# Rank products directly behind the mask's wait, three units' column sums behind the ranks, in a routed two-layer block kernel

## The reference, cut to what matters

```python
def hierarchical_moe(hin, w_group, b_group, w_router, b_router, w_gate, w_up, w_down):
    ...
    g_w, g_idx = lax.top_k(g_prob, 1)
    ...
    e_val, e_idx = lax.top_k(e_logits, EXPERT_TOP_K)
    e_w = jax.nn.softmax(e_val, -1)
    flat_idx = g_idx * EXPERTS_PER_GROUP + e_idx
    ...
    for e in range(N_EXPERTS):
        hid = jax.nn.silu(xt @ w_gate[e]) * (xt @ w_up[e])
        y = y + gates[:, e:e + 1] * (hid @ w_down[e]).astype(jnp.float32)
```

## Time and profile before

| | us |
|---|---|
| median of three timed runs | 1268.32 |
| lowest and highest of them | 1265.24, 1273.74 |
| the profiled execution | 1266.25 |
| its span | 1264.5 |
| mean granted clock of PE in it | 0.979 |

### The profile page before, as it was taken

One profiled execution on the slowest core, in us unless ns is written; L12 is line 12 of the kernel. 1 busy time (PEld: TensorE's weight loads), 2 busy tenths in 40 slices (PEclk: granted clock), 3 DMA queues, 4 the chain that ended last, 5 costly groups with the idle time before them and its releaser, 6 DMA issues.

```text
span 1264.5 us, 17438 instructions
## 1 busy us (share of the span) xinstructions
PE 1198.5 (95%) x7154; PEld 702.5 (56%) x7155; DVE 361.2 (29%) x1017; ACT 295.0 (23%) x626; POOL 83.8 (7%) x141
## 2 busy tenths in 40 slices
PE   4799999999999999999889999999999999999997
PEld 1566644544444448764433444445878778767773
DVE  0202414322212123952521121114211344342212
ACT  2112433111000021063400000103002545542101
POOL 2000011000000001500000000000000313200000
PEclk8799999899999999999989999999999999999999
DMA  9997999999999999831889999999834433424000
GB/s 336 313 387 243 308 280 385 382 425 428 430 429 428 429 397 208 247 133 67 360 355 404 404 422 429 427 429 388 204 133 146 152 97 130 150 80 145 17 1 33
DMA packets 90371, 352.77 MB, mean 279 GB/s; under 512 B 5284, under 2 KB 7500, under 8 KB 78028
## 3 DMA queue, kind: packets, MB, share of 16 engines
q1 hardware_dynamic: 83160, 340.68, 71.6%
q0 software_dynamic: 5488, 8.12, 3.1%
q10 hardware_dynamic: 1668, 3.21, 0.7%
HBM read 350.84 MB, written 1.15 MB: 278 GB/s over the span
## 4 chain that ended last, share of the span: by engine, by line
PE 80%; DMA 13%; DVE 2%; ACT 2%; issue 2%; SPq 1%; ACTq 0%; DVEq 0%
PE bank L456 28%; PE bank L751 20%; PE bank L469 12%; DMA ring<-in_moe_w_up 10%; PE bank L723 3%; PE bank L492 3%; PE bank L772 3%; DMA ring<-in_ev_w_in 2%; PE bank L505 2%; PE bank L1016 1%; SPq L368 1%; PE bank L603 1%; PE bank L640 1%; PE bank L643 1%; PE bank L629 1%
## 5 line engine op out<-in xcount | busy, mean ns | idle before, releaser
L456 PE MATMUL bank<-arena,ring 128*128 128x256 f32 x1600 | 356.0, 384 | 6.1 <-DVE arena L1539 2.8
L751 PE MATMUL bank<-ring,arena 128*32 128x512 f32 x3072 | 339.5, 600 | 12.1 <-issue 7.1
L456 PEld LDWEIGHTS bank<-arena,ring 128*128 128x128 f32 x1600 | 305.7, 192 | 54.6 <-issue 7.1
L751 PEld LDWEIGHTS bank<-ring,arena 128*32 128x32 f32 x3072 | 102.0, 111 | 237.0 <-issue 234.3
L469 PE MATMUL bank<-ring,arena 128*128 128x512 f32 x352 | 153.7, 594 | 2.3 <-DVE arena L2378 1.5
L469 PEld LDWEIGHTS bank<-ring,arena 128*128 128x128 f32 x352 | 66.2, 190 | 83.0 <-issue 79.6
L492 PE MATMUL bank<-ring,c_rep 128*32 128x512 f32 x480 | 64.3, 667 | 11.8 <-DMA ring<-in_w_ada 10.1
L2003 DVE TENSOR_TENSOR arena<-arena,bank 128x512 f32<-128x512 f32 x16 | 11.0, 688 | 203.8 <-PE bank L751 203.8
L723 PEld LDWEIGHTS bank<-arena 128*128 128x128 f32 x512 | 60.3, 197 | 13.6 <-issue 13.3
L723 PE MATMUL bank<-arena 128*128 128x128 f32 x512 | 63.4, 284 | 1.6 <-DVE arena L1971 1.5
L1283 ACT ACTIVATE arena<-bank 128x512 f32<-128x512 f32 x16 | 9.6, 597 | 216.8 <-PE bank L751 216.8
(11 more groups left out here) (300 smaller groups left out, 926.5 us busy)
## 6 DMA issues: line engine op xcount, KB each, us to landing
ring<-in_moe_w_gate SPq DMA_DIRECT2D x32, 2048.0 KB, 14.0
ring<-in_moe_w_up SPq DMA_DIRECT2D x32, 2048.0 KB, 16.7
ring<-in_moe_w_down SPq DMA_DIRECT2D x32, 2048.0 KB, 13.8
ring<-in_w_ada SPq DMA_DIRECT2D x24, 2048.0 KB, 14.1
ring<-in_w_in SPq DMA_DIRECT2D x16, 2048.0 KB, 8.9
ring<-in_w_c SPq DMA_DIRECT2D x6, 2048.0 KB, 9.2
ring<-in_ev_w_in SPq DMA_DIRECT2D x5, 2048.0 KB, 20.2
ring<-in_od_w_in SPq DMA_DIRECT2D x5, 2048.0 KB, 19.6
```

What stands on the lines that cost most here:

```text
L456: mm = pe.matmul(ps[k0][:, t * S:(t + 1) * S], w[:, k, c:c + P], rhs[:, k, :], start=(k == 0), stop=(k == KT - 1))
L751: mm = pe.matmul(bank[col:col + CHUNK, :], lhs[:, k, col:col + CHUNK], ring[:, s0 + e, cut], start=start, stop=stop, tile_position=(0, col))
```

## The change

In `experts` of the PE program the wait for `ada_part_taken` and the three `ada_columns` move from ahead of the wait for `mask_ready` to behind the five rank products, ahead of the last `ada_main`. No instruction is added or taken away, and no other engine's program changes. It takes effect twice, once in each layer.

```diff
                 for n in range(units - 3):
                     ada_main()
-                pe.wait_ge(sem("ada_part_taken"), units_before + 4)
-                for n in range(ROUTE_SOON):
-                    ada_columns()
-
                 pe.wait_ge(sem("mask_ready"), layer + 1)
                 mask = rt[:, 512:512 + 32].rearrange("p (t e) -> p t e", e=EXPERTS)
                 pe.matmul(ps[4][:, 384:400], lt, mask[:, 0, :], start=True, stop=True)
...
                 pe.matmul(ps[4][:, 416:432], ones, mask[:, 0, :], start=True, stop=False)
                 pe.matmul(ps[4][:, 416:432], ones, mask[:, 1, :], start=False, stop=True)\
                   .then_inc(sem("rank_full"), 1)
+                pe.wait_ge(sem("ada_part_taken"), units_before + 4)
+                for n in range(ROUTE_SOON):
+                    ada_columns()
                 ada_main()
```

## The result

The changed kernel takes 1272.01 us (median of 20 executions, 1266.21 to 1275.46) against 1268.41 for the kernel before (20 executions, 1264.84 to 1273.74). The ratio is 1.0025, 95% interval 1.0014 to 1.0037: by this ratio 3.2 us slower, between 1.8 and 4.7 (the two medians themselves lie 3.6 apart). The forecast was 1.5 us slower, the rival in which the clock falls in layer 1 as well 3.2 to 5.2 (1271.5 to 1273.5).

The account below looks back on a forecast made before the run. PE was taken to hold 80% of the span and arriving weights 13%. Layer 1's +0.1 and layer 0's +1.4 gave +1.5 us, 1267.75 for the profiled execution and 1269.8 as median (chance 0.36); range 1264.0 to 1276.0.

Parts of the forecast that it names:

- the rival in which the clock falls in layer 1 as well: Layer 1's last modulation product, perhaps its gather too, runs at half clock: 1271.5 to 1273.5, written 1272.5; chance 0.24.
- The wait for the mask: PE ahead of the ranks, both layers: without the columns' cover it idles 1.24 us, bounds 1.1 and 1.5.
- DVE: In layer 1 ranks start 1.43 us earlier and so do the picks; DVE's wait shrinks from 2.82 to about 1.4.
- The copy takes the place of the picks: Ahead of the gather, ACT's copy of the last part, 1.24 us later in layer 1, becomes the last wait.
- the rival that said they would: Early ranks get through to the gather: layer 1 gains 1.43 us, layer 0 0.3; 1266.6, chance 0.09.
- Layer 1's +0.1, at full clock: Layer 1's gather, with no clock fall, starts at 626.23 instead of 626.12: net +0.1 us.
- The cases without any fall: Clock falls in neither layer: +0.1 in layer 1 and -0.3 in layer 0, 1268.1; chance 0.18.
- without any effect: Layer 1's stall ends at a fixed time and layer 0's queue has more reserve: 1268.3; chance 0.10.
- The stall of 4.08 us: PE's wait ahead of layer 1's first pair, no releaser shown; taken to move with PE, so the 0.1 stays.
- Layer 0's +1.4: Clock falls and returns as before; gather ends at 237.73 instead of 236.35, +1.4 us; bounds -0.3 and +1.4.
- the queue passes the lateness on in full: Weight stream sets each layer's end: a later first pair delays it fully; an earlier one gains about 0.3 us in layer 0.
- Theory A: From the experiments: the time is PE at half clock, as idleness, ranks and columns side by side bring more or earlier falls.

Follow-up runs that it names:

- four filled ones: Changed kernel with one 512-column product (ratios 0.9990, 0.9989) or five one-column products (1.0075, 1.0077) ahead of the mask's wait, results unused; each run twice.
- layer 1 alone: New order in layer 1 only, layer 0 as in the kernel before: 1270.04 us, ratio 1.0015 to the kernel before.
- changed, again: The changed kernel, unaltered, run a second time: 1271.59 us against 1266.88 for the kernel before, ratio 1.0026.
- layer 0 alone: New order in layer 0 only, layer 1 as in the kernel before: 1269.19 us against 1266.96, ratio 1.0015.
- four products first: Changed kernel with the last modulation product moved ahead of the mask's wait, behind its three sisters: 1266.28 us against 1268.39 for the kernel before, ratio 0.9983.
- the same, again: Last modulation product moved ahead of the mask's wait in the changed kernel, second run: 1266.27 us against 1266.88 for the kernel before, ratio 0.9986.
- and one dense product: Four products first, plus one unused 512-column product behind the first unit's columns: 1265.01 us against 1266.88 for the kernel before, ratio 0.9989.
- before, with dense product: Kernel before with one unused 512-column product between columns and ranks: 1268.41 us against 1268.39, ratio 0.9999.
- dense product in the wait: Changed kernel with one unused 512-column product ahead of the mask's wait: 1264.81 us against 1266.96 for the kernel before, ratio 0.9990.
- one unit ahead: Changed kernel with one of the three units' columns kept ahead of the mask's wait: 1267.11 us against 1268.39 for the kernel before, ratio 0.9985.
- dense in the wait, again: Changed kernel with one unused 512-column product ahead of the mask's wait, second run: 1267.22 us against 1268.39 for the kernel before, ratio 0.9989.

## Why the prediction was right or wrong

The range held, the direction was right, and the size was short: 1.5 us forecast, 3.2 measured, with 1.5 just below the interval of 1.8 to 4.7. The steps in their order:

*The wait for the mask.* Forecast 1.24 us of idleness; 1.17 in both layers. Right.

*DVE.* The ranks were to come 1.43 us earlier; they came 1.46 earlier (12.28 to 10.82), and DVE's wait shrank to 1.38, as forecast. Right.

*The copy takes the place of the picks.* Right in both layers: the picks were done 5.5 us ahead of the gather in layer 1 and 4.2 in layer 0 (228.53 to 232.73), and ACT's L1172 released it. This is why nothing of the early ranks got through, and the rival that said they would is refuted. The sum of +0.1 at full clock was never seen, since no stage of the new order ran without a fall.

*Layer 1's +0.1, at full clock.* This is the step that failed. It supposed that layer 1 would keep the full clock it had in the one profile before. All 14 profiled stages with the whole change, the wait filled or not, had a fall in them (two in each of the two profiles of the changed kernel and of the four filled ones, one in each single-layer run), and so had all ten stages of the orders tried besides; only the old order had stages without one, two of four. The gather came 3.95 us later, where the prediction allowed 0.3, and the first pair 6.35. That profile is the worst of its kind. In layer 1, against 17.24, 26.00 and 271.62 us from the logits before:

| profile | clock in the stage | gather late by | first pair late by | experts over late by |
|---|---|---|---|---|
| changed | fall | 3.95 | 6.35 | 4.83 |
| changed, again | fall | 3.37 | 3.84 | 1.39 |
| layer 1 alone | fall | 3.37 | 3.78 | 1.31 |
| layer 0 alone (layer 1 in the old order) | fall | 1.62 | 3.81 | 1.69 |

So the old order with a fall ended its layer 1 as late as the new order did in two of its three profiles. The one profile before, on which the forecast was built, had no fall in this place, and the forecast also left out the fall under the first pair, of which the 0.91 from 640 to 645 was a sign. The rival with this mechanism, 1271.5 to 1273.5, holds the measured 1272.01. The cases without any fall (1268.1) and without any effect (1268.3) lie below the interval.

*The stall of 4.08 us* ahead of layer 1's first pair moves with PE, as taken: 4.20 after, and 4.47 with layer 1 alone; over all profiles it is 3.7 to 4.6. In the kernel before a transfer of instructions lies within it, between 631 and 632 us; its cause was not tried.

*Layer 0's +1.4.* The first pair was 1.22 us later, near the forecast, but not by the recorded steps. They let the clock fall at the old time, under the columns, which would take 4.84 us, and start the gather 21.24 us from the logits. The fall came 1.22 us later, the columns took 3.63 and the gather started at 19.86. The end comes out alike because the same 10.24 us of half clock lay inside the stage either way, and only the new idleness was added. In three other profiles the fall in the stage was longer (changed, again and layer 0 alone: 13.6 us) or missing (layer 1 alone), and the first pair moved with it. That the queue passes the lateness on in full was not borne out by the changed profile. Against 25.23 and 261.59 in the kernel before:

| profile | first pair, from the logits | experts over | late by | came through |
|---|---|---|---|---|
| layer 1 alone (old order, no fall) | 21.84 | 260.99 | -3.39 | -0.60 |
| four products first | 23.43 | 260.80 | -1.80 | -0.79 |
| the same, again | 23.83 | 261.09 | -1.40 | -0.50 |
| and one dense product | 24.06 | 260.80 | -1.17 | -0.79 |
| before, with dense product | 24.53 | 260.73 | -0.70 | -0.86 |
| dense product in the wait | 25.06 | 262.64 | -0.17 | 1.05 |
| one unit ahead | 25.56 | 262.60 | 0.33 | 1.01 |
| changed | 26.45 | 262.04 | 1.22 | 0.45 |
| dense in the wait, again | 26.46 | 262.44 | 1.23 | 0.85 |
| changed, again | 28.08 | 263.72 | 2.85 | 2.13 |
| layer 0 alone | 28.08 | 263.76 | 2.85 | 2.17 |

Of the largest lateness three quarters come through; of an earlier pair 0.9 us at the most, whatever it gains, where 0.3 was forecast. Between them a pair that is 0.9 us later (changed against one unit ahead) has its experts over 0.6 us sooner, and one that is 0.5 us later (dense product in the wait against before with it) 1.9 us later. These profiles do not show why, so a reserve of the queue can't be read off to a microsecond. A fall that comes early enough in layer 0 is in any case not hidden, and the run with layer 0 alone puts its price at 1.9 us (0.3 to 3.5).

*A number.* The prediction says that all named cases lie within 5.3 us. From the median of 1268.3 the farthest lies 5.2 away, but from the first case to the last it is 6.9 us.

So the mechanism of the prediction (copy instead of picks, then the clock) was right; its likeliest case was built on the clock of one execution. The range held because it was drawn over the rival with a fall in layer 1 as well, not by the forecast's own case. Theory A stands for the sum, by the dense filler, with the moved code as the rival that no run excludes. How the price divides between more falls, earlier falls and longer ones is not settled by single profiles.

## What to carry to other kernels

A change of order by a microsecond or two on TensorE can be priced by where it leaves idleness beside work of few columns, and not by the waits alone: compare mean granted clocks over many executions, and do not take the clock of one profile for the kernel's. Ahead of a wait that has lost its cover, put the dense product that is needed anyway: here that made a loss of 3 us into a time no worse than before. Check which wait comes second before making the first one shorter.

## What the runs showed of the hardware that was not expected

Identical instructions of one stage took 17.2 us from logits to gather at full clock and 18.6 or 18.9 with a fall, in different layers and different executions. The page "TensorE: Matmul & The Clock Gate" of the Trainium skill (Part 1, The HAM clock gate) says that the monitor runs freely against the kernel and that slow matmuls vary from run to run; the spread of the kernel before, 1261.8 to 1273.7 us over its runs, with mean clocks between 0.973 and 0.985, agrees with it. With five one-column products more in each layer a stall of 5.5 us appeared some 250 us behind those of layer 0, in front of products that the edit does not touch, in both executions that were profiled; that the moved code is its cause is likely and not shown.

A stall can bring a fall of its own. In layer 1 of the kernel before PE stood idle from 630.80 to 634.88 us and the clock was low from 634.06 to 640.90, under the products behind the stall. The stall ahead of layer 1's first pair had such a fall behind it in 12 of the 14 profiles of this case, 3.4 or 6.8 us long. A stall can thus cost more than the idle time that the page prints.
